# A hybrid decoder step on one core: the samples' branches joined in two parts, the joining stage in a planned order, and layer norms on a provisional mean

## The reference

```python
z = x @ w_in            # split in four head groups
A  conv module          # GLU, causal depthwise conv, LayerNorm, swish, pointwise
B  NSA, 4 heads         # compressed blocks, selected blocks, window of 512; gated sum
C  MoBA, 4 heads        # blocks of 256 keys, top 3 by q.mean(k), plus the own block
D  causal pooling
x = layer_norm(ALPHA * x + concat(A, B, C, D) @ w_out)
x = layer_norm(ALPHA * x + square(relu(x @ w_up)) @ w_down)      # width 4096 inside
```

## Time and profile before

| what | us |
|---|---|
| median of 3 runs (lowest, highest) | 918.35 (916.82, 925.22) |
| the profiled execution | 918.73 |
| its span, first to last instruction | 915.8 |
| mean granted clock of TensorE | 0.953 |
| busy: PE / DVE / ACT / POOL | 815.5 / 396.3 / 277.7 / 85.6 |

### The profile page before, as it was taken

The page is one execution under the profiler, slowest core; times in us unless marked ns, Lnnn a source line. Parts: engine busy times, 40 slices in busy tenths (PEclk is TensorE's granted clock), DMA queues, the critical chain, the costliest instruction groups (busy, mean ns, idle before and its releaser), DMA issues.

```text
span 915.8 us, 17217 instructions
## 1 busy us (share of the span) xinstructions
PE 815.5 (89%) x6889; PEld 702.5 (77%) x6889; DVE 396.3 (43%) x732; ACT 277.7 (30%) x552; POOL 85.6 (9%) x107
## 2 busy tenths in 40 slices
PE   6999899688866887898997599999999999999993
PEld 6988777565432433476996499999999999999992
DVE  3289953355664442532424733333233323333226
ACT  4322134244454222211213333331233123311104
POOL 0004360000000000000000711110011001100000
PEclk9999999779979899999899899999999999999997
DMA  9456663524558794023232033333223333333202
GB/s 328 135 142 165 175 168 123 208 93 147 189 177 289 221 295 125 12 70 117 71 109 98 23 93 92 93 93 93 93 92 92 93 93 92 93 93 93 70 1 93
DMA packets 73289, 113.18 MB, mean 124 GB/s; under 512 B 25177, under 2 KB 42202, under 8 KB 72538
## 3 DMA queue, kind: packets, MB, share of 16 engines
q1 hardware_dynamic: 65146, 110.26, 38.4%
q10 hardware_dynamic: 8064, 1.84, 0.9%
HBM read 107.63 MB, written 6.52 MB: 125 GB/s over the span
## 4 chain that ended last, share of the span: by engine, by line
PE 75%; DVE 12%; ACT 4%; DMA 2%; issue 2%; SPq 2%; POOL 2%; ACTq 1%; DVEq 0%
PE psum L617 53%; DVE yc L1358 4%; PE psum L695 2%; POOL xres L1255 2%; PE psum L727 2%; PE psum L920 2%; PE psum L877 2%; PE psum L626 2%; PE psum L961 2%; PE psum L670 2%; PE psum L970 1%; PE psum L866 1%; PE psum L698 1%; SPq L471 1%; PE psum L905 1%
## 5 line engine op out<-in xcount | busy, mean ns | idle before, releaser
L617 PE MATMUL psum<-opH,wH 128*128 128x260 f32 (+1 forms) x928 | 196.2, 293 | 32.6 <-DVE opL L1665 13.9
L617 PE MATMUL psum<-opL,wH 128*128 128x260 f32 (+1 forms) x928 | 190.1, 287 | 0.0
L617 PE MATMUL psum<-opH,wL 128*128 128x260 f32 (+1 forms) x928 | 189.5, 286 | 0.0
L617 PEld LDWEIGHTS psum<-opH,wH 128*128 128x128 f32 (+1 forms) x928 | 146.4, 192 | 45.4 <-issue 22.3
L1002 ACT ACTIVATE wH<-raw 128x1024 fp32r<-128x1024 f32 x90 | 93.9, 1043 | 184.0 <-PE psum L617 179.4
L617 PEld LDWEIGHTS psum<-opL,wH 128*128 128x128 f32 (+1 forms) x928 | 145.7, 192 | 0.4
L617 PEld LDWEIGHTS psum<-opH,wL 128*128 128x128 f32 (+1 forms) x928 | 145.2, 191 | 0.4
L1296 DVE TENSOR_TENSOR wL<-raw,wH 128x1024 fp32r<-128x1024 f32 x90 | 109.1, 1212 | 52.0 <-ACT wH L1002 52.0
L617 PE MATMUL psum<-hidH,wH 128*128 128x260 f32 x512 | 104.1, 284 | 0.0
L617 PE MATMUL psum<-hidH,wL 128*128 128x260 f32 x512 | 103.2, 283 | 0.0
L617 PE MATMUL psum<-hidL,wH 128*128 128x260 f32 x512 | 103.1, 283 | 0.0
(11 more groups left out here) (305 smaller groups left out, 899.8 us busy)
## 6 DMA issues: line engine op xcount, KB each, us to landing
raw<-in_panels SPq DMA_DIRECT2D x89, 512.0 KB, 3.6
moba_lo<-in_moba_pages SPq DMA_DIRECT2D x64, 256.0 KB, 3.8
moba_hi<-in_moba_pages SPq DMA_DIRECT2D x64, 256.0 KB, 3.9
nsa_ring<-in_nsa_pages SPq DMA_DIRECT2D x128, 96.0 KB, 2.2
selV<-in_selv_pages SPq DMA_DIRECT2D x72, 32.0 KB, 2.4
xres<-in_xT SPq DMA_DIRECT2D x8, 260.0 KB, 5.5
xres<-in_xT SPq DMA_DIRECT2D x1, 2080.0 KB, 8.4
out_y<-xres SPq DMA_DIRECT2D x8, 260.0 KB, 2.2
```

The lines of the kernel that those rows point to most:

```text
L617: last = mm(out[0:M, hf, 0:HALF], w, x[:, k, hf * HALF:(hf + 1) * HALF], start=(t == 0 and j == 0), stop=(t == KT - 1 and j == 2))
```

## The change

Two parts, and the order of steps around them.

**The joining stage.** `stat` and `comb` are split: `stat 0` to `4`, `comba`, `backa` treat the selected and window branches, `statm`, `combm`, `backm` the MoBA branch. A sample is `psc b` (the scaling by DVE), `st b 0..2` (its transposes in three steps, all through bank 2) and `spv b` (the products, which wait for that sample's own semaphore of selV). `fin` is split likewise into `fina` and `finm`; `msplit 4, 5` follow the first, `6, 7` the second. `lse` is cut in two (`lse`, `lset`). `spread` over groups is replaced for this stage by a list of (time, step) pairs which `merged` sorts. Units start at `MU1` = 10 instead of 11; `win` and `mu 0` move into the pieces of panel 15. Two `selv` steps go with each unit, all 32 by unit 25; the last sample's values have a place of their own. The instructions of the matmuls are otherwise the same.

**The norms.** `mean` and the old `ln` are gone. `xsum` (POOL) adds tiles 0 and 1, `smean` multiplies this with the 1/1024 matrix: four times that is the provisional mean. DVE subtracts it from tiles 0 to 2 after their evacuation and, for tiles 3 to 7, before it (`pre`). ACT squares each tile (`xs`), POOL sums tiles and squares (`dsum`, `qsum`); one product with 1/1024 for each sum gives the error d of the mean and the variance (`ln`, `lnv`). For norm 1 the ups multiply `oxH/oxL` = g x (x - provisional mean), with two more columns b and g; an up is corrected at its evacuation by the reciprocal deviation and by d times the g column (DVE), then relu and square on ACT. `x1` (POOL, two operations a tile) and `x1a` (ACT) bring `xres` itself up to date during ups 0 to 9. For norm 2 centring is shared by DVE and POOL, DVE multiplies by the reciprocal deviation, and ACT applies gain and b. The feed-forward panels use three pairs of banks.

```diff
+    head = [(0, ("out_z", 0)), (0.1, ("zrow", 2)), (0.2, ("own", 0)), (1.5, ("vrow", 0)), (2.5, ("vrow", 1)), (3, ("msplit", 0)), (3, ("msplit", 1))]
+    rows = [(0.5 + 0.8 * n, ("row", NR0 + n)) for n in range(NR - NR0)]
+    rows += [(0.3, ("lse", 0)), (5.5, ("lset", 0)), (7, ("lse", 1)), (13, ("lset", 1))]
+    for u in range(MU1, MU + 1):
+        at_ = 1 + UNIT * (u - MU1)
+        units += [(at_, ("mu", u)), (at_ + UNIT / 2, ("mp", u - 1))]
+        units += [(at_, ("selv", k)) for k in (2 * (u - MU1), 2 * (u - MU1) + 1) if k < 4 * B]
+    end = 1 + UNIT * (MU + 1 - MU1)
+    join = [(9 + 2 * k, ("stat", k)) for k in range(5)] + [(18.5, ("comba", 0)), (20, ("comba", 1)), (29, ("backa", 0))]
+    for b in range(B):
+        at_ = 33 + (end - 40) / B * b
+        join += [(at_ - 3, ("psc", b))] + [(at_ + 1.7 * c, ("st", b, c)) for c in range(3)] + [(at_ + 6, ("spv", b))]
...
     for i in range(OUT0, FF0):
-        tl += panel(i, [("mean", 0, i - OUT0 - 1)] if i > OUT0 else [])
-    tl += [("mean", 0, KT - 1), ("ln", 0)]
+        tl += panel(i, [("smean", 0)] if i == OUT0 + 2 else []) + tail(0, i - OUT0)
     for i in range(FF0, N_PANELS):
         k = i - (N_PANELS - KT)
-        tl += panel(i, [("mean", 1, k - 1)] if k > 0 else [])
-    tl += [("mean", 1, KT - 1), ("ln", 1)]
+        step = panel(i, [("smean", 1)] if k == 2 else [])
+        if i == FF0:
+            at_ = step.index(("evac", i))
+            step[at_:at_] = [("ln", 0), ("split", i + 2), ("lnv", 0)]
+        if i == FF0 + 1:
+            step.remove(("split", i + 1))
+        tl += step + (tail(1, k) if k >= 0 else [])
+        if i - FF0 < KT:
+            tl.append(("x1", i - FF0))
+        if 0 <= i - FF0 - 2 < KT:
+            tl.append(("x1a", i - FF0 - 2))
...
+PAIR = [1 if NACC0 <= n < NACC1 else n % 2 if n < NACCF else (0, 1, 3)[(n - NACCF) % 3] for n in range(len(ACC))]
...
 # scalar, evacuation of an up
+                    act.wait_ge(up_t, up_no + 1)
+                    fn(relu[:, up_no % 2, :], relu[:, up_no % 2, :], ACT.Relu, bias=wcol[:, up_no % 3, 0:1], scale=-1.0).then_inc(relu_done, 1)
...
 # vector, evacuation of an up
+                        nc.vector.tensor_copy(wcol[:, up_no % 3, :], src[:, 1, HALF:HALF + 2]).then_inc(wcol_done, 1)
+                        tt(zview(buf), src[:, :, 0:HALF], zview(std[:, :]), ALU.mult).then_inc(acc_read[1], 1)
+                        stt(buf, dmul, wcol[:, up_no % 3, 1:2], buf, ALU.mult, ALU.subtract).then_inc(up_t, 1)
...
 # gpsimd, x1
+                    nc.gpsimd.tensor_tensor(xres[:, n, :], xres[:, n, :], dmean, ALU.subtract).then_inc(ln_e, 1)
+                    nc.gpsimd.tensor_tensor(xres[:, n, :], xres[:, n, :], std[:, :], ALU.mult).then_inc(ln_m, 1)
```

More of the change, by code:

```diff
@@ L20 @@
 HALF = NT // 2
+NX = NT + 2
 H, HD = 4, 64
@@ L123, in pieces, with merged @@
         out = [s for s in panel(i) if s[0] not in ("mm", "evac")]
-        out += spread([[("mm", i, q, n), ("row", first + q)] for q in range(n)], extras)
+        out += spread([s for q in range(n) for s in (("mm", i, q, n), ("row", first + q))], extras)
         return out + [("evac", i)]
+    def merged(*streams):
+        steps = [s for stream in streams for s in stream]
+        return [s for _, s in sorted(steps, key=lambda p: p[0])]
     nt = 2 * CW
@@ L170, in timeline @@
         if i == 14:
[L171 to L177, removed]
@@ L190, in timeline, with tail @@
+    tl += merged(head, rows, units, join, cols, last)
+    def tail(n, m):
+        out = {1: [("xsum", n)]}.get(m, [])
+        out = out + [("pre", n, k) for k in {2: (3, 4), 3: (5,), 4: (6, 7)}.get(m, ())]
+        return out + [("xs", n, k) for k in {2: (0,), 3: (1, 2), 4: (3, 4), 5: (5,), 6: (6,), 7: (7,)}.get(m, ())]
     for i in range(OUT0, FF0):
-        tl += panel(i, [("mean", 0, i - OUT0 - 1)] if i > OUT0 else [])
-    tl += [("mean", 0, KT - 1), ("ln", 0)]
+        tl += panel(i, [("smean", 0)] if i == OUT0 + 2 else []) + tail(0, i - OUT0)
@@ L232 @@
 USES = [[], [], [], []]
-for _s in [s for s in TL if s[0] in ("zrow", "vrow", "csc", "ctr", "cimp", "win", "mu", "mp", "stat", "back", "spv", "mpv", "fin", "lse")]:
-    _k, _n = _s
-    _banks = {"csc": (0,), "ctr": (1,), "cimp": (0, 1), "win": (0, 1), "back": (0, 1), "fin": (0, 1)}.get(_k, ())
+for _s in TL:
+    _k, _n = _s[:2]
+    _banks = {"csc": (0,), "ctr": (1,), "cimp": (0, 1), "win": (0, 1), "mp": (1,), "stat": (2,), "backa": (2,), "st": (2,), "fina": (2,),
+              "statm": (0, 1, 2), "backm": (2,), "mpv": (1, 2), "finm": (1,)}.get(_k, ())
     if _k in ("zrow", "vrow"):
@@ L310, in build, with centred @@
         lnt = place("lnt", [P, 4, NT], F32, o_after_hid + 7 * NT * 4)
+        xsum, qsum, dmul, dmean = (lnt[:, q, :] for q in range(4))
+        def centred(eng, n, k):
+            if k < 3:
+                eng.wait_ge(ln_d, 3 * n + k + 1)
+            else:
+                read(eng, ("mm", (OUT0, N_PANELS - KT)[n] + k))
+        wcol = place("wcol", [P, 3, 2], F32, o_after_hid + 11 * NT * 4)
         zc = place("zc", [P, 2, CW - 1 + T], F32, o_m)
@@ L925, in _ @@
                     mm(out, wnew[:, 2, b, :], zs[:, 2, HD:P], start=False, stop=(b == B - 1), skip_group_check=True).then_inc(spv_mm, 1)
+                elif kind == "fina":
+                    bank(2, step)
+                    pe.wait_ge(fin_o, 1)
+                    for c in range(2):
+                        last = nc.tensor.transpose(psum[0:HD, 2, c * P:(c + 1) * P], On[:, c, :], ident)
+                    last.then_inc(fin_mm, 1)
                 elif kind == "mpv":
```

668 lines of the change are left out of this document (391 added, 277 removed).

## The result

The changed kernel takes 884.8 us, median of 4 runs (883.1 to 887.36), beside 918.18 of the kernel before on the same chip: ratio 0.9624, 95% interval 0.957 to 0.9678. A second set, beside other experiments, gave 884.99 and 0.9642 (0.9578 to 0.9706). The forecast was 847 with a range of 826 to 880. So the change is faster, as forecast, but it gains 33 us where 72 were summed, and the time lies above the range.

The account below looks back on a forecast made before the run. TensorE work bounds the feed-forward stage; the other stages hold idle time and lower clock. Gains 8 + 30 + 2.3 + 24.8 - 2.6 + 3.6 + 5.9 = 72 off 915.8, plus 2.9, gave 847 us, range 826 to 880.

Parts of the forecast that it names:

- B: Joining stage: samples of the selected and window branches join while units run; 185 us becomes 155, a gain of 30.
- I keep half the idle: Joining stage: samples as cover halve the 36.5 us of TensorE idle to 18, giving 155 us.
- The floor of 137: Joining stage: 148.5 us busy, less 13 for full clock, plus 1.5 for unit 10.
- The price of bank 2: Joining stage: 24 sample transposes and 5 statistics use one bank, each waiting for its reader; range ends 142 and 178.
- The slower rival: Joining stage: every bank 2 step finds its reader behind an ACT burst; stage 247 us, time 939; chance 0.04.
- The rival of pacing by issues: Joining stage: ACT's and SP's issues and bank 2 pace it; stage 178 us, time 870; chance 0.22.
- A: Panels 15 to 17: win and mu 0 moved behind row pieces, unit 10 leaves panel 17; gain 8 us, ends 0 and 12.
- C: w_out: seven means leave, one smean comes, stalls of 2.5 and about 0.5 us; gain 2.3 us.
- D: Norm 1: ups start on uncorrected x without a gap, stall of 1.9 us ahead of up 3; gain 24.8 us.
- E: The ups: longer evacuations hidden by slack except in eight panels, two more columns at 0.02 us each; costs 2.6 us.
- F: Last eight downs: seven means leave, one smean comes, stall of 1.7 us in panel 3; gain 3.6 us.
- G: Norm 2: 24.4 us from the last matmul to the end becomes 18.5; gain 5.9 us.

Follow-up runs that it names:

- e9: Changed kernel with fina ahead of the statistics and weights of m, and the exponential of m's weights behind two columns: 877.98 us, ratio 0.9541.
- e16: Changed kernel with the copy PTw on DVE instead of ACT: 878.6 us, ratio 0.9566.
- e14: Changed kernel with e9's edits, row sums unhooked, rows 3.0 apart, selV four units later, mean tails behind the splits, PTw on DVE: 857.34 us, ratio 0.9329.
- e11: Changed kernel with extra matmuls that nothing reads in the first 42 us of the joining stage: 887.06 us, ratio 0.9636.
- e1: Changed kernel with all selV load steps issued by SP and none by ACT: 895.83 us, ratio 0.9764.
- e7: Changed kernel with win and mu 0 back behind panel 14: 894.57 us, ratio 0.973.
- e13: Changed kernel with the joining stage in the old order and a sample's three transpose groups in three banks: 887.42 us, ratio 0.9672.

## Why the prediction was wrong, point by point

**B.** This is the term that failed. It came out 37.7 us short; the errors of all other terms cancel within 2 us, by luck. The stage was to have 137 us of TensorE's work and 18 of idle; it has 160.1 and 36.8. So 19 us of the miss are idle and 23 are busy time, 3 of these because my stage began later (the last point). Four steps failed.
- "I keep half the idle." The argument was that columns and samples would cover the waits. Idle stayed at 36.8 us instead of 18. Cover helps only where the queue that holds the late instruction is not itself the one that waits; I had listed the waits on the one bank, but not ACT's wait for the row sums (4.6), `On` behind the weights of m (6.7) or `PTw` behind the bursts. e9 and e16 removed about 7 us each.
- The floor of 137 took all matmuls at full clock. No variant's stage ran above 0.93; this one has 0.86. Of 196.9 us, 28% are at 1.2 GHz, 55 us, worth at most half of that. In e14, with several waits gone, the stage idles 21.5 us, near the 18 that I forecast, and still has 154.4 us of busy time, at a clock of 0.90. By my estimate 20% of its 175.9 us at 1.2 GHz are worth at most 17.6, just what lies over the floor. So the floor is right as a sum of matmuls, and what it left out is the clock. In the first stretch e11 raised the clock and gained nothing.
- The price of bank 2 was left at the ends of the range with "16 of 24 are read by DVE". Measured: 15.7 us in the old order, as much as the order gains. And the eight that ACT reads cost about 7 us. The slower rival had the right mechanism (a reader behind a burst) and the wrong size: three waits of TensorE for it stand in the trace, not 24.
- I put the start of the stage at 249.5; the last input matmul had ended at 245.3. So the old stage was 189.2 and not 185, and 3.0 of these 4.2 us are busy: 4 us of the 42 between 155 and 197 are this boundary and no wait.

The experiments go as far as e14 and no further: its 175.9 us are still 17 to 21 above the forecast, and how the clock could be kept up in this stage is open.

The rival of pacing by issues (178, 870) was nearer in size (with the 68 us that B leaves for the rest of the stage, where the rival has 59, it comes to 187 and 879; the 3.1 us a MB in B's bytes are 3.2 by the earlier trace rows, which changes no term), and half right in mechanism: SP is near its limit (e1), but ACT's issues cost by their place and not by their sum: all 64 are still on ACT in e14, whose stage is 175.9.

**A.** Forecast 8, of which 1.5 are unit 10 and 6.9 the placement; e7 measured 8 to 10 for the placement alone. The 15.4 of the traces hold, besides, unit 10 and differences between executions: the last input matmul ends from 227.3 to 239.0 in profiles whose code up to there is the same.

**C.** Gain 1.7 for 2.3, but not by its own sum. The stall ahead of panel 5's matmuls was to be 2.5 and is 3.3, and panel 5 itself, behind the stall, takes 1.6 us longer at a lower clock, a term that C does not have. What hides this is the first w_out panel: in the kernel before it came behind the late waits of the joining stage (TensorE was busy 1.25 of the last 4.45 us), ran at a clock of 0.65 and took 8.55 us to the next panel; now it takes 5.79. These 2.8 us come from the order of the joining stage, B's part, and not from the means: e13, with the new norms and the old order, has 8.3 there. The windows of the first panel before, then of panels 5 and 6 after, and of the same place in the last downs:

```profile
434.45:443.16 8.71, 8.71 (x50) 8.71 (x51) 3.75 (x5) 3.07 (x5) 0.00 (x0) 0.65 0.22 63
```

```profile
460.13:467.63 7.50, 7.50 (x50) 7.50 (x51) 6.73 (x6) 2.21 (x3) 5.72 (x4) 0.77 0.26 72
467.46:473.33 5.87, 5.87 (x52) 5.87 (x51) 3.75 (x3) 2.21 (x3) 3.05 (x2) 1.00 0.31 89
845.40:852.89 7.49, 7.49 (x50) 7.49 (x51) 3.04 (x4) 1.59 (x2) 5.91 (x4) 0.77 0.00 1
```

**D, E, F.** 17.6 for 25.8. No gap stands between w_out and up 0, as forecast. The stall ahead of up 3 is 3.2 for 1.9 (the listed steps of D's chain add up to 14.8 and not 14.2, which alone makes it 2.5), and up 3 behind it takes 7.4 us, 1.6 more than other ups. Six ups (5 to 10), beside `x1` and `x1a`, take 6.08 to 6.10, and the ups after them 5.83, where I had 6.0 and 5.77: some twenty ups with 0.06 for the two more columns, where E had 0.02. F's term was mis-sized most. The evacuations of the last downs:

```profile
837.02 0.70 DVE L1775 SCALAR_TENSOR_TENSOR xres<-xres,psum 128x520 f32<-128x520 f32 x1 [0.72 <-PE psum L653]
...
840.41 1.30 POOL L1342 TENSOR_TENSOR lnt<-sqb 128x520 f32<-128x520 f32 x1
...
841.80 0.64 ACT L1259 ACTIVATE sqb<-xres 128x520 f32<-128x520 f32 x1 [2.06 <-POOL lnt L1342]
...
843.42 1.88 DVE L1397 TENSOR_TENSOR wL<-raw,wH 128x1024 fp32r<-128x1024 f32 x1 [3.75 <-ACT wH L1057]
844.17 2.29 POOL L1338 TENSOR_TENSOR lnt<-lnt,xres 128x520 f32<-128x520 f32 x1
845.22 0.68 DVE L1775 SCALAR_TENSOR_TENSOR xres<-xres,psum 128x520 f32<-128x520 f32 x1
...
852.93 0.70 DVE L1775 SCALAR_TENSOR_TENSOR xres<-xres,psum 128x520 f32<-128x520 f32 x1 [4.05 <-PE psum L653]
```

The panels take 8.2 and 7.7 us instead of 5.77, 4.4 us more where 1.7 stood: TensorE stands still for 2.65, and the panel behind the stall takes 1.6 more at a clock of 0.77. I had priced POOL's additions at 1.05, from the square; with inputs from two tiles they are 1.30. And `wL` took 1.88 beside them, not 1.22. The low clock behind the stalls of up 3 and of the last downs is 3.2 of the 8.2 us that D, E and F are short, and it was a term of none of them.

**G.** 18.7 for 18.5, and each step of it: squares and means to 3.7 after the last matmul, reciprocal of 3.39, eight products in 4.97. The five centrings on POOL took 1.25 each, not 1.05, and stood in nobody's way.

```profile
870.70 3.39 DVE L1817 RECIPROCAL std<-std 128x520 f32<-128x520 f32 x1
874.12 4.97 DVE L1825 TENSOR_TENSOR xres<-xres,std 128x520 f32<-128x520 f32 x8
874.86 5.80 ACT L1273 ACTIVATE xres<-xres,vec 128x520 f32<-128x520 f32 x8 [5.13 <-DVE xres L1825]
```

What worked was the part where each instruction was laid on its engine's line one by one: G, and the place and cause of each stall, though every stall was priced too low. What failed was the part done with shares and averages (B).

## What to carry to other kernels

When stages are interleaved by a plan, each engine's queue gets the plan's order too: for every step that waits for a slow chain, look at what stands behind it on that same engine, on both engines of the chain, and give the waiting half a step of its own. A short instruction that frees a shared buffer does not belong on an engine that also issues loads in bursts. And more overlap that must be paid with fewer buffers has to be priced by both: here the order gained 13 us, and the single bank cost as much where it could be measured. Last, a stall between matmuls that are otherwise the bound costs more than its length: here each of about 3 us had 1.6 us of lower clock behind it.

## What the runs showed of the hardware

A DVE operation with two SBUF inputs and a POOL addition shut each other out for nearly their whole length in the rows here, which I had discounted in the forecast. With POOL running from 439.27 for 1.31, `wL` took 2.01:

```profile
439.27 1.31 POOL L1332 TENSOR_TENSOR lnt<-xres 128x520 f32<-128x520 f32 x1 [306.50 <-DVE xres L1747]
439.65 2.01 DVE L1397 TENSOR_TENSOR wL<-raw,wH 128x1024 fp32r<-128x1024 f32 x1 [0.46 <-ACT wH L1057]
```

It ended 1.08 after POOL did, nearly its whole length of 1.23. In the rows at 843.42 the two alternate: `wL` waits for POOL, then the next addition takes 2.29 for 1.30. The evacuation at 845.22, which reads one input from PSUM, took 0.68 beside POOL, as alone. That is what the Trainium skill says (SBUF — State Buffer, "Who interferes with whom": outside VectorE's two-port modes, contention only for a DVE instruction with two SBUF inputs, and then an exclusive lock); the trace agrees, and the 0.4 us that I had taken from the earlier trace rows was too small.

A POOL addition of 128x520 takes 1.30 us when its inputs are two tiles, and 1.05 as a square of one tile. Two shifted views of one tile, 510 columns, take 1.03, so it is not the number of inputs alone. The kernel before already had one at 1.30 in its trace.

Extra matmuls in idle gaps raised the granted clock of a stretch from 0.68 to 0.82 without making it shorter or, for 63 more matmuls, longer by more than 0.7 us. After each of the three stalls of 2.65 to 3.3 us between panels the next panel's granted clock was 0.77 to 0.78 and it took 7.5 us, where its neighbours took 5.9 to 6.0 at 1.00.
